# Head 0's k, q and v blocks ahead of the gated convolution blocks in layers 3 and 4

## The reference

```
px = hx @ w_in            # conv_x (a, g), q, k, v, gate logits; hx = modulated rmsnorm(x)
q, k = rope(rmsnorm(q)), rope(rmsnorm(k))        # 8 heads x 2 maps x 64
w = softmax(q1 k1) - lam * softmax(q2 k2)        # per head
attn = rmsnorm(w @ v) * (1 - lam_init)           # v is 128 wide per head
z = a * sigmoid(g)                               # GLU, 512 channels
z = depthwise_conv(z, 31 taps) + b_dw ; y_conv = silu(layernorm(z)) @ w_conv_out
y = (sig(g1) * y_conv + sig(g2) * (attn @ w_attn_out)) @ w_out
```

## Time and profile before

| | |
|---|---|
| median of three executions | 2640.07 us |
| the profiled execution, first to last instruction | 2646.0 us |
| mean granted TensorE clock in it | 0.941 of full |
| PE, DVE, ACT busy in it | 2376.6, 1424.6, 1082.0 us |
| layer 3: first matmul of the first pair to first normalisation of head 0 | 1080.72 to 1175.78 us |
| layer 3: first normalisation of head 0 to that of head 4 | 1175.8 to 1320.8 us |
| layer 4: first matmul of the first pair to first normalisation of head 0 | 2053.01 to 2118.80 us |

### The profile page before, as it was taken

One profiled execution on the slowest core, in us unless ns is written; L12 is line 12 of the kernel. 1 busy time (PEld: TensorE's weight loads), 2 busy tenths in 40 slices (PEclk: granted clock), 3 DMA queues, 4 the chain that ended last, 5 costly groups with the idle time before them and its releaser, 6 DMA issues.

```text
span 2646.0 us, 34404 instructions
## 1 busy us (share of the span) xinstructions
PE 2376.6 (90%) x13550; PEld 1873.4 (71%) x13550; DVE 1424.6 (54%) x2364; ACT 1082.0 (41%) x1826; POOL 32.2 (1%) x40
## 2 busy tenths in 40 slices
PE   5798999999878999879979899899998788989999
PEld 2355677777656888656548577588887666769899
DVE  4255433333655544798863634544434977656665
ACT  4153422212544333435564432423323455654543
POOL 0300000000010000000000000000000000000000
PEclk8898999999999999889989899899999898989999
DMA  6800444444314777325502122333222211225454
GB/s 258 292 33 32 144 143 144 145 135 141 132 46 160 261 248 241 118 80 191 187 24 92 48 74 91 114 103 104 91 92 96 80 64 44 96 69 182 150 183 146
DMA packets 94879, 335.87 MB, mean 127 GB/s; under 512 B 10624, under 2 KB 12672, under 8 KB 94464
## 3 DMA queue, kind: packets, MB, share of 16 engines
q1 hardware_dynamic: 94720, 333.67, 37.2%
HBM read 332.58 MB, written 1.05 MB: 126 GB/s over the span
## 4 chain that ended last, share of the span: by engine, by line
PE 71%; DVE 15%; ACT 6%; DMA 4%; issue 3%; SPq 0%; ACTq 0%; DVEq 0%
PE out L996 21%; PE out L997 20%; PE out L998 20%; DMA raw<-stream 4%; DVE stage L1557 3%; PE sc L976 2%; DVE w_lo L1322 2%; PE pv L1073 2%; PE aux L1006 2%; PE sc L1051 1%; DVE smax L1506 1%; PE pt L1061 1%; ACT w_hi L1107 1%; ACT e_t L1228 1%; DVE rs L1449 1%
## 5 line engine op out<-in xcount | busy, mean ns | idle before, releaser
L996 PE MATMUL out<-act_hi,w_lo 128*128 128x512 f32 (+1 forms) x2272 | 814.4, 358 | 58.3 <-DVE act_lo L1460 46.0
L997 PE MATMUL out<-act_lo,w_hi 128*128 128x512 f32 (+1 forms) x2272 | 793.6, 349 | 0.0
L998 PE MATMUL out<-act_hi,w_hi 128*128 128x512 f32 (+1 forms) x2272 | 792.0, 349 | 0.0
L1107 ACT CAST w_hi<-raw 128x1024 fp32r<-128x1024 f32 (+2 forms) x444 | 452.6, 1021 | 494.3 <-PE out L998 433.1
L1322 DVE TENSOR_TENSOR w_lo<-raw,w_hi 128x1024 fp32r<-128x1024 f32 (+2 forms) x444 | 529.2, 1197 | 199.7 <-ACT w_hi L1107 199.3
L996 PEld LDWEIGHTS out<-act_hi,w_lo 128*128 128x128 f32 x2272 | 443.6, 195 | 149.7 <-issue 87.1
L998 PEld LDWEIGHTS out<-act_hi,w_hi 128*128 128x128 f32 x2272 | 442.1, 195 | 52.9
L997 PEld LDWEIGHTS out<-act_lo,w_hi 128*128 128x128 f32 x2272 | 443.9, 195 | 50.3 <-issue 0.5
L996 PE MATMUL out<-mix_hi,w_lo 128*128 128x256 f32 (+1 forms) x1184 | 403.0, 340 | 4.1 <-DVE mix_lo L1344 2.1
L997 PE MATMUL out<-mix_lo,w_hi 128*128 128x256 f32 (+1 forms) x1184 | 398.9, 337 | 0.0
L998 PE MATMUL out<-mix_hi,w_hi 128*128 128x256 f32 (+1 forms) x1184 | 398.5, 337 | 0.0
(11 more groups left out here) (146 smaller groups left out, 1784.4 us busy)
## 6 DMA issues: line engine op xcount, KB each, us to landing
raw<-stream SPq DMA_DIRECT2D x604, 512.0 KB, 3.8
raw<-stream SPq DMA_DIRECT2D x16, 384.0 KB, 4.1
raw<-stream SPq DMA_DIRECT2D x16, 256.0 KB, 3.0
x<-xin SPq DMA_DIRECT2D x1, 2048.0 KB, 11.6
consts<-const SPq DMA_DIRECT2D x1, 1344.0 KB, 8.3
x<-ctx SPq DMA_DIRECT2D x1, 1024.0 KB, 5.7
out<-x SPq DMA_DIRECT2D x8, 128.0 KB, 1.7
consts<-const SPq DMA_DIRECT2D x1, 320.0 KB, 11.4
```

What stands on the lines that cost most here:

```text
L996: nc.tensor.matmul(ps, wl, xh, start=(k == 0), stop=False)
L997: nc.tensor.matmul(ps, wh, xl, start=False, stop=False)
L998: ins = nc.tensor.matmul(ps, wh, xh, start=False, stop=(k == s.nk - 1))
L1107: nc.scalar.copy(w_hi[:, number % HL, 0:n], raw[:, place[number] % RAW, 0:n]).then_inc(S["hi_ready"], 1)
```

## The change

The loop over the four pairs becomes a function `glu_block(t)` without taps, and head 0's steps are written out by hand. k and q are the pair that follows the norm together; since in layer 4 k has 512 columns and q 256, the matmul loop now cuts its activation operand to the columns of the block at hand. The pairs of the convolution are set between the steps of head 0, and the taps behind them.

```
-        for t in range(4):
+        def glu_block(t):
             g = w("w_cg", t, n, "sg", func=ACT.Sigmoid)
             g.qg, g.qg_free = take("sgl", 2, None)
             a = w("w_ca", t, n, "glu", other=g, free=last.get(("cz", 0)))
-            if t == 0:
-                together(g, a)
             last["sgl", g.qg] = a.rel
             glu.append(a)
-            conv_taps(8)
...
-        for f in head_work(0):
-            f()
-            conv_taps(4)
+        q_block, k_block, q_norm, q_done, v_block, k_norm, k_done, v_turn = head_work(0)
+        k_block()
+        q_block()
+        together(held["k", 0], held["q", 0])
+        v_block()
+        q_norm()
+        glu_block(0)
+        q_done()
+        k_norm()
+        conv_taps(3)
+        glu_block(1)
+        k_done()
+        v_turn()
+        conv_taps(6)
+        glu_block(2)
+        conv_taps(8)
+        glu_block(3)
+        conv_taps(12)
...
-                        xh = hi[:, s.k0 + k, 0:s.n]
-                        xl = lo[:, s.k0 + k, 0:s.n]
                         for g in group:
                             assert g.n <= s.n and g.nk == s.nk
+                            xh = hi[:, s.k0 + k, 0:g.n]
+                            xl = lo[:, s.k0 + k, 0:g.n]
```

More of the change, by code:

```diff
@@ L530, in conv_taps @@
             todo = []
-            for _ in range(count):
+            for _ in range(count if glu else 0):
                 t = min(range(len(glu)), key=lambda t: (taps_done[t], t))
```

## The result

The changed kernel takes 2650.8 us (median, 2648.5 to 2656.7), against 2640.7 us of the kernel before on the same chip (2636.1 to 2645.2): a ratio of 1.0043, 95% interval 1.0026 to 1.0059. It is slower by about 10 us. The forecast was 2647 with a range of 2632 to 2661, and the measured time lies in it. Two executions ran far slower at a low granted clock (3920.5 us at 0.554 of the kernel before, 3055.5 us at 0.732 of taps_only), and medians and ratios leave them out.

What follows compares the result with a forecast made beforehand. DVE was taken as the bound from layer 3's first pair to head 4. Layer 3 +7.8, layer 4 -0.5 and clock +0.5 gave +7.8 us, rounded to +7: 2647 us against a median of 2640.07, range 2632 to 2661.

Steps and rivals of the forecast that it cites:

- The start of layer 3: Up to head 0's first normalisation: 22.4 us less tap work, 12.4 us more waits, so 10.0 us earlier.
- The new waits: DVE's waits at layer 3's start under the new order: 21.2 us together against 8.8, 12.4 more.
- PE's wait for the exponential: Layer 3's start: PE stands 7 us for the first exponential, since 12 taps lie ahead of the maximum.
- The heads of layer 3: Heads 0 to 3: eight more taps per head, six on the chain at 0.66 us each; 16.8 us longer in all.
- So DVE, not PE, is the bound from the first pair to head 4: Layer 3: DVE's chain decides the time, read from the chain through head 1, with six of eight taps on it.
- The check from the other side: Layer 3's head 3, with fewer taps, was 2.05 us shorter than heads 1 and 2's mean: 0.29 us a tap.
- rival 1: The heads hide about half of the taps, 0.29 us each; 2640 us, chance 0.20.
- DVE would be busy over 92%: Sign to look for in layer 3's heads 0 to 3, each lasting 3 to 5 us longer.
- 5.5 us won at the end of head 0: Layer 4: head 1's first turn on DVE 7.2 us earlier, less 1.7 for taps in two groups on the chain.
- rival 3: The clock decides: PE falls to the lower level in each of seven heads, 14 us more; 2661 us, chance 0.15.
- Rival 4: Alternating tables and rstd/sigmoid order hold ACT, so head 0 starts 3 us earlier instead of 10; 2654 us, chance 0.07.
- Rival 2: The heads hide nearly all taps and the start's gain stays; 2627 us, chance 0.08.

Runs made afterwards that it cites:

- taps_only: Kernel before with its old block order, but 35 taps of a layer early instead of 70; 2649.4 us, ratio 1.0030 (profiled again in one run, 2648.2 us).
- order_only: Changed kernel's new order in layers 3 and 4, but 70 taps early as in the kernel before; 2662.6 us, ratio 1.0080.
- all_early: Kernel before, old order, with all 124 taps of a layer ahead of the first scores; 2682.2 us, one run.
- before_again: The kernel before, run once more with no edit; 2643.3 us, ratio 1.0001.
- l4_only: New order in layer 4 alone, layer 3 as in the kernel before; 2644.3 us, ratio 1.0008.
- mid8: Kernel before, old order, 54 taps early instead of 70: 8 behind each pair, 2 behind each step of head 0; 2639.8 us, ratio 0.9985.
- after_again: The changed kernel, run once more with no edit; 2655.2 us, ratio 1.0050.
- l3_only: New order in layer 3 alone, layer 4 as in the kernel before; 2648.7 us, ratio 1.0026.
- norms_first: Changed kernel with q's norm ahead of v's block and k's rstd ahead of the first gate block; 2654.6 us, ratio 1.0051.
- pairs8: Kernel before, old order, 35 taps early: 8, 8, 8, 5 behind the four pairs, none behind head 0's steps; 2643.9 us, ratio 1.0014.
- no_sigmoid_table: Changed kernel with the gate's sigmoid in layers 3 and 4 replaced by a square, which needs no other table; 2645.4 us, ratio 1.0010.

## Why the prediction was right, and where it was not

**The start of layer 3: right.** Forecast 10.0 us earlier; measured 98.5 - 87.8 = 10.7, and 10.3 in the second pair of runs. The new waits were summed to 12.4 us, and DVE waits 22.8 - 10.4 = 12.4 us more in the window. order_only shows the same sum by itself, 12.1 us. The single waits came near: the longest, by the first sigmoid, was put at 4.0 and is 4.1 us, the last at 3.8 and is 3.78. PE's wait for the exponential, put at 7, is 6.9. Each of the nine summed waits of DVE came within 0.4 us of its estimate.

**The heads of layer 3: the sum right, the reason not.** Forecast +16.8 us for heads 0 to 3; measured 163.9 - 145.0 = 18.9, and 163.2 - 146.5 = 16.7. (Head 1 grew by 5.7 us, more than the 3 to 5 that the prediction gave each.) That the sum came out is partly luck: the wrong step would have shown only if taps had been taken out, or fewer put in. The failing step is the sentence "So DVE, not PE, is the bound from the first pair to head 4", and with it the bounds of a straight line, 0.66 us for each tap on the chain. By taps that are left to the heads and the start of head 4 (4 to 8 of them stand in head 4 or ahead of the first normalisation), heads 0 to 3 together take:

| taps left | kernels | heads 0 to 3 | us for each tap more |
|---|---|---|---|
| 0 | all_early | 144.9 | |
| 54 | before, before_again, order_only, l4_only | 145.4 (144.2 to 146.5) | 0.01 |
| 70 | mid8 | 151.0 | 0.35 |
| 89 | changed, after_again, l3_only, norms_first, taps_only_b, pairs8 | 163.3 (161.7 to 164.0) | 0.65 |

(0.01 is 145.4 - 144.9 over 54 taps, and so on.) The first 54 cost nothing, since PE covers them; the next 16 about half of a tap's 0.66 us; the last 19 nearly all of it. Head by head the knee is sharper, since `taps_due` does not spread the taps evenly:

| kernel | taps in heads 0, 1, 2, 3 | their lengths, us |
|---|---|---|
| all_early | 0, 0, 0, 0 | 33.4, 37.7, 37.7, 36.1 |
| before | 14, 14, 14, 8 | 34.1, 37.8, 37.5, 35.6 |
| mid8 | 20, 15, 14, 14 | 37.7, 37.9, 37.5, 37.9 |
| changed | 22, 22, 22, 15 | 38.7, 43.5, 41.7, 40.0 |

mid8 leaves heads 1 and 2 as they were, with one tap more between them, and pays in heads 0 and 3, to which it gives six each: 3.6 and 2.3 us (0.7 us against before_again's head 3 of 37.2). So heads 0 to 2 hide about 14 taps each, and the kernel before stands right at the knee in heads 0 to 2. There the chain of waits shows one of two chains of about the same length. Through head 1 of before, its line of shares begins with DVE:

```profile
by line: DVE stage L1557 16.0%; DVE w_lo L1322 9.2%; DVE smax L1506 8.4%; DVE rs L1449 5.6%; ACT e_t L1228 5.3%; DVE e_t L1522 4.6%; issue 4.4%; DVE e_t L1521 3.7%; DVE sq L1448 3.5%; PE pt L976 2.9%; PE sc L1051 2.9%; ACT w_hi L1107 2.5%; 
```

Through head 1 of all_early, equally long, there is no step of DVE on it:

```profile
by line: PE out L1000 15.2%; PE out L1002 14.5%; PE out L1001 14.5%; PE pt L980 14.3%; PE sc L1055 9.7%; PE pv L1077 9.3%; PE aux L1010 6.9%; PE pt L1065 5.2%; PE pt L1013 2.7%; issue 1.9%; ACT rs L1190 1.8%; ACT ms L1192 1.5%; ACT v_t L122
```

Which of the two is shown is an accident of the execution. Through head 1 of before_again, the same kernel and 38.0 us long, PE's work leads:

```profile
by line: PE pt L976 11.3%; PE out L998 9.7%; PE out L996 9.6%; PE out L997 9.6%; PE pv L1073 7.4%; PE sc L1051 6.5%; PE aux L1006 4.6%; issue 3.9%; PE pt L1061 3.8%; DVE smax L1506 3.4%; ACT rs L1186 3.3%; ACT ms L1188 3.0%; DVE w_lo L1322 
```

The prediction also took head 1's chain for all four heads. In the trace that it read, the taps' share is 16.0% in head 1, but 7.1% in head 2 and 3.7% in head 3. Here is head 2's line:

```profile
by line: PE pt L976 7.6%; DVE stage L1557 7.1%; DVE smax L1506 6.7%; DVE w_lo L1322 6.3%; issue 5.6%; ACT e_t L1228 5.3%; PE sc L1051 5.1%; PE out L998 4.9%; PE out L996 4.9%; PE out L997 4.9%; PE pv L1073 4.7%; PE aux L1006 4.6%; DVE e_t L
```

What PE waited for in head 1 of before, next to nothing, says the same:

```profile
PE pt L1061 <- ACT v_t L1217: 1.6, 1, 1.6
PE pt L1061 <- DVE e_t L1522: 0.2, 1, 0.2
```

PE was 36.0 of 37.8 us busy and waited 1.8: it was the bound. DVE's chain was as long, so adding to it cost at once, and taking from it gave nothing in all_early. In the changed kernel the same window has PE waiting 6.4 us:

```profile
PE pt L1074 <- DVE e_t L1535: 4.9, 3, 2.1
PE pt L1074 <- ACT v_t L1230: 1.3, 1, 1.3
PE pt L989 <- DVE stage L1381: 0.2, 1, 0.2
```

and in the chain the taps stand in twos, in seven of the eight groups (two of them here, and the three of a turn):

```profile
1202.05 1.32 DVE stage L1570 x2
...
1212.17 1.32 DVE stage L1570 x2
...
1219.91 2.08 DVE stage L1570 x3
```

The group right behind the first normalisation, which I had covered by PE's transposes, is now on the chain; the one behind the second still isn't. Taps have 6.0 us of head 1's chain before (nine of them, 16.0% of 37.8) and 11.3 after (seventeen): 5.3 us more, for a head 5.7 us longer. (The view's share after, 27.6% of 43.5, is 12.0 us, with a tap that begins ahead of the window.) The check from the other side, 0.29 us a tap by head 3, was a reading of PE's time, as I had written, and rival 1, built on it, fell for that reason. (It was also misread: head 3 had six taps fewer than heads 1 and 2, 8 for 14, which makes 0.34.) That DVE would be busy over 92% was wrong too: it is 88% (38.13 of 43.50). At the bound by a chain that crosses two engines, neither is full.

**Head 4 of layer 3.** Start and heads together: 251.7 - 243.5 = 8.2 and 251.3 - 244.9 = 6.4 us later; the forecast for layer 3 with head 4's share was 7.8. At head 5 it is 8.2 and 7.7.

**Layer 4.** The first normalisation comes 3.0 us earlier (69.2 to 66.2; 3.8 in the second pair), as forecast. Then the step "5.5 us won at the end of head 0" was too large. Head 1's first turn on DVE does come 6.4 us earlier behind the norm (forecast 7.2), but head 1's first normalisation only 95.9 - 92.6 = 3.3. The 3.1 us between are four groups with two more taps each, near 0.8 us a group: in head 0 all four stand between that turn and head 1's first normalisation, where the forecast counted two. Heads 1 to 3 lose 3.3 + 2.1 = 5.4 us (forecast 5.0), and head 4 comes 2.1 us later, 3.5 in the second pair, where 0.5 earlier was forecast. At the layer's end 1.7 and 0.6 us are left.

**The clock: small in layer 3, the open part of layer 4.** The granted clock is 0.92 to 0.96 in heads 0 to 3 of layer 3 where 0.95 to 1.00 before, and the scores at 1158.47 take 2.08 us, the time of the lower level. Head 1 takes 43.5 us at a clock of 0.92 and 42.4 at 1.00 (taps_only_b) with as many taps: 1.1 us at most. Some of PE's slow pieces are on head 1's chain there: transposes, sum of squares and turned copy take 1.11, 1.71 and 0.83 us where they took 0.66, 0.86 and 0.53 in before. In layer 4 the clock costs more. The changed kernel and l4_only have the same steps there; head 1:

```profile
2140.90:2172.80 31.90, 27.59 (x125) 21.08 (x125) 25.42 (x57) 15.60 (x34) 0.00 (x0) 0.84 0.15 50
2140.50:2170.90 30.40, 25.02 (x124) 19.37 (x123) 25.41 (x56) 15.32 (x33) 0.00 (x0) 0.94 0.16 53
```

DVE works as long in both, and PE 2.6 us longer at the lower clock. Heads 1 to 3 take 90.7 us in the changed kernel and 87.6 in l4_only, and that is nearly all of the 3.2 us by which head 4 comes later (183.4, 180.1). With l4_only's clock the forecast for head 4, 0.5 us earlier than before, would have come near (before has 181.3 and 179.8). So rival 3, which asked for 14 us, fell in its size; about 3 us of it are there. Whether the clock falls oftener because of the change isn't shown: before has 0.87 to 1.00 in these heads. The oscillation that the Trainium skill describes (page "TensorE: Matmul & The Clock Gate", section "HAM oscillation — how this bites in real kernels") shows here as a clock that falls to the lower level once or twice in each of heads 1 to 3 of layer 3 (at 1215.0, 1235.5, 1259.4 and 1300.4 us) and comes back.

**Rival 4** fell: head 0 does start 10 us earlier. Rival 2 fell with rival 1.

**The end.** Forecast +7, measured +10 (interval of the ratio: 7 to 16 us). The worked sum was +7.8 and was rounded down to +7, not up. Part of the rest is layer 4, 1 or 2 us at its end where 0.5 won was forecast. The time from layer 3's norm to the next norm went from 609.1 to 612.1 us in one pair of traces and from 607.3 to 616.5 in the other. From head 6's start to head 7's last item it is 47.0 us in the changed kernel's first trace and 50.7 to 51.0 in the other three; runs of other kernels show both lengths. The prediction named a move of over 3 us in another stretch as a sign against it; the first pair has one here, of 3.8 us less, and the second has not. What sets it stays open, and so the last 2 or 3 us do too.

**Why the change doesn't pay.** It aims at 16.8 us of idle PE. They are not won by blocks that come earlier but by less work on DVE ahead of head 0: taps_only_b has this without the order. And the work comes back in heads that PE already fills: in layer 3 of that kernel 12.4 us are won at the start and 16 lost in the heads. The new order puts waits of DVE, 14 of its 22.8 us, ahead of the first GLU, when there are no taps yet to fill them. mid8 moves only 16 taps: they give 8.6 us at the start of layer 3 and cost 5.2 in its heads.

## What to carry to other kernels

Ahead of moving work from a stage with idle time to a full one, ask of the full stage both ways: which engine never waits there, and how long is the chain of the engine that gets the work. If they tie, the first pieces moved cost nearly their whole length (six taps in head 0 cost 0.6 us each), while pieces taken away give nothing; the chain alone shows only one of the two, and another execution may show the other. And a chain read in one head is not the chain of its neighbours. Try the split of a filler in two or three sizes before trying an order: in the old order 16 taps moved came out 0.15% faster (interval 0.02 to 0.28), 35 moved 0.1 to 0.3% slower. And an order of blocks is judged by what can fill its waits: the same steps cost 12 us more where the filler depended on blocks that came later.

## What the runs showed of the hardware

- A table load takes 1.28 us, with the next step 0.02 us behind it (1155.58, 1156.88). Taking out four of them moved the first normalisation by 2.1 to 2.4 us in layer 3 and 1.0 in layer 4. A load with no idle time ahead of it (1140.14 in before) starts 0.02 us behind the eviction before it.
- Head 1 of layer 3 with 22 taps took 42.4 us at a granted clock of 1.00 (taps_only_b), 42.4 to 43.0 at 0.96 (pairs8, no_sigmoid_table, after_again) and 43.5 at 0.92. Head 1 of layer 4 took 30.4 us at 0.94 and 31.9 at 0.84, DVE's work being equal.
